# Three plain blocks at the start of the up projection with its differences on VectorE, six banks in the down projection, and output gates later in the chunk steps

## The reference

```python
m = W_out [ retention group | HGRN2 group | sliding-window attention group ](x @ w_in)
x = layernorm(ALPHA * x + m)
h = relu(x @ w_up)                              # w_up is 1024 x 4096
x = layernorm(ALPHA * x + (h * h) @ w_down)     # w_down is 4096 x 1024
```

## Time and profile before

| | |
|---|---|
| median of three executions | 2855.7 us (2853.38 to 2856.41) |
| the profiled execution | 2851.14 us |
| its span | 2849.0 us |
| PE / PEld busy | 2586.0 us (91%) / 2396.6 us (84%) |
| DVE / POOL / ACT busy | 1709.1 us (60%) / 1075.5 us (38%) / 834.9 us (29%) |
| mean granted clock of PE | 0.954 of full |

### The profile page before, as it was taken

The page is one execution under the profiler, slowest core; times in us unless marked ns, Lnnn a source line. Parts: engine busy times, 40 slices in busy tenths (PEclk is TensorE's granted clock), DMA queues, the critical chain, the costliest instruction groups (busy, mean ns, idle before and its releaser), DMA issues. The chain is left out here.

```text
span 2849.0 us, 45428 instructions
## 1 busy us (share of the span) xinstructions
PE 2586.0 (91%) x18174; PEld 2396.6 (84%) x18174; DVE 1709.1 (60%) x3360; ACT 834.9 (29%) x1668; POOL 1075.5 (38%) x1090
## 2 busy tenths in 40 slices
PE   6998888787899999999899988887978999999996
PEld 6997776586899999999899877666868999999986
DVE  2136668557756566666751366785586555666668
ACT  2235456321222221111122445562322222211110
POOL 0027456635455532222000456664535555222220
PEclk9999999888999999999999999997989999999998
DMA  4442222152133352322343422321512333532223
GB/s 156 144 153 82 84 75 76 40 174 78 61 109 103 104 183 91 94 91 91 102 142 127 160 81 68 103 65 30 178 67 88 102 110 99 180 97 91 91 76 108
DMA packets 225889, 295.84 MB, mean 104 GB/s; under 512 B 28816, under 2 KB 177616, under 8 KB 225648
## 3 DMA queue, kind: packets, MB, share of 16 engines
q1 hardware_dynamic: 225680, 292.94, 32.1%
HBM read 217.27 MB, written 77.66 MB: 104 GB/s over the span
## 5 line engine op out<-in xcount | busy, mean ns | idle before, releaser
L1081 PE MATMUL ps<-hid_hi,wd_hi 128*128 128x256 f32 (+2 forms) x800 | 259.3, 324 | 19.9 <-DVE acc_a L2733 13.1
L1081 PE MATMUL ps<-hid_hi,wdl_hi 128*128 128x256 f32 (+2 forms) x800 | 257.8, 322 | 0.0
L1082 PE MATMUL ps<-hid_lo,wdl_hi 128*128 128x256 f32 (+2 forms) x800 | 256.3, 320 | 0.0
L1083 PE MATMUL ps<-hid_hi,wdl_lo 128*128 128x256 f32 (+2 forms) x800 | 256.2, 320 | 0.0
L1082 PE MATMUL ps<-hid_lo,wd_hi 128*128 128x256 f32 (+2 forms) x800 | 255.6, 320 | 0.0
L1083 PE MATMUL ps<-hid_hi,wd_lo 128*128 128x256 f32 (+2 forms) x800 | 255.6, 320 | 0.0
L3038 POOL TENSOR_TENSOR wq_lo_S<-ws,wq_hi_S 128x512 fp32r<-128x512 f32 x112 | 209.2, 1877 | 107.4 <-ACT wq_hi_S L2059 107.4
L2717 DVE TENSOR_TENSOR acc_a<-ps,acc_a 128x512 f32<-128x512 f32 x208 | 143.8, 692 | 152.3 <-PE ps L1083 152.3
L2987 POOL TENSOR_TENSOR wl_lo<-wl_raw,wl_hi 128x2048 fp32r<-128x2048 f32 x14 | 63.8, 4554 | 449.2 <-ACT wl_hi L1772 449.1
L2717 DVE TENSOR_TENSOR acc_b<-ps,acc_b 128x256 f32<-128x256 f32 (+1 forms) x416 | 178.2, 439 | 77.4 <-PE ps L1083 72.1
L1081 PE MATMUL ps<-t_hi_T,wq_hi_S 128*128 128x256 f32 (+1 forms) x672 | 193.2, 288 | 20.0 <-issue 20.0
(11 more groups left out here) (329 smaller groups left out, 7991.9 us busy)
## 6 DMA issues: line engine op xcount, KB each, us to landing
wd_raw<-in_w_down SPq DMA_DIRECT2D x32, 1024.0 KB, 4.9
wq_raw<-in_w_up SPq DMA_DIRECT2D x28, 1024.0 KB, 6.3
wl_raw<-in_w_in SPq DMA_DIRECT2D x20, 1024.0 KB, 5.2
wi_raw<-in_w_in SPq DMA_DIRECT2D x15, 1280.0 KB, 6.4
hidscr<-h SPq DMA_DIRECT2D x32, 544.0 KB, 8.0
out_y<-xn SPq DMA_DIRECT2D x32, 512.0 KB, 4.2
hidscr<-h SPq DMA_DIRECT2D x32, 512.0 KB, 7.2
hid_raw<-hidscr SPq DMA_DIRECT2D x32, 512.0 KB, 3.5
```

The lines of the kernel that those rows point to most:

```text
L1081: nc.tensor.matmul(out, a_hi, b_hi, start=start, stop=False)
L1082: nc.tensor.matmul(out, a_hi, b_lo, start=False, stop=False)
L1083: return nc.tensor.matmul(out, a_lo, b_hi, start=False, stop=stop)
```

## The change: what it does

**Up.** Block 2 becomes a third plain block: `PLAIN = 3`, six more units, 13 blocks of seven products instead of 14. POOL's `side` is gone; DVE makes all four differences and lows of both sides, in an order written anew among the squares. `split_wu(2)` puts the third block's high part on ACT and low part on POOL, each in two halves, into the buffers of block 0. SP loads it ahead of the first quarters. `rectify` of block 2 writes over block 0's h, and waits until that is saved. **Down.** Six banks instead of three; the lows of block 15 are spread over parts 0 and 1. **Chunk steps.** `gates_clip(f)` stands behind `heads_keys` of the chunk's own step, the ACT chain of three (`gates_out`) behind that step's `front_copies`, `front_silu` behind `heads_weights`, and POOL's product with the norm's weights behind `levels`. In step 4 POOL runs `rotate(g)` behind `levels`.

```diff
-         (1, 0, 2), (1, 1, 2), (0, 0, 2), (0, 1, 2)]
+         (0, 0, 2), (0, 1, 2), (1, 0, 2), (1, 1, 2)]
+PLAIN = 3
+UNITS += [(2, f, c) for f in range(2) for c in range(TCH)]
-SEVENS = FBLOCKS - 2
+SEVENS = FBLOCKS - PLAIN
...
# SP
-                load_quarters(l, 2)
+                load_wu(l, 2)                    # waits for wu_hi_done and wu_lo_done of block 0
+                load_quarters(l, PLAIN)
...
+                save_h(l, 0, 1)
                 save_h(l, 1, 1)
-                save_h(l, 0, 1)
...
# PE, up_unit: lows of tokens awaited at the first unit of each token range
+                if b == 0 and f == 0:
                     pe.wait_ge(sd.sem, sd.at("lo", split_no(l, 0, (3, 5, 8)[c])))
# PE, feed
+                for unit in UNITS[8:]:
+                    up_unit(l, *unit)
+                for b in range(PLAIN, FBLOCKS):
                     up(l, b)
# PE, down
-                        if i >= 3:
-                            pe.wait_ge(down_free, n - 2)
+                        if i >= 6:
+                            pe.wait_ge(down_free, n - 5)
...
-                            last = three(ps[:, i % 3, 0:CW[c]], ...
+                            last = three(ps[:, i % 6, 0:CW[c]], ...
# PE, down_last: the first three units
-                        pe.wait_ge(xd.sem, xd.at("h1", seven_no(l, FBLOCKS - 1)))
+                        pe.wait_ge(down_free, DOWN * l + 334 + i)
# ACT, gates
                     nc.scalar.activation(g_r[:], g_r[:], ACT.Ln).then_inc(gh.step("f"), 1)
+
+                def gates_out(c):
                     act.wait_ge(gc.sem, gc.at("c1", c.n))
                     nc.scalar.activation(gate[c.p][:], gate[c.p][:], ACT.Exp, scale=-1.0).then_inc(gh.step("eg"), 1)
...
                         front_copies(f)
+                        gates_out(f)
                     dense(step, "a1")
# ACT, rectify
+                if b == 2:
+                    act.wait_ge(h_saved[0][c > 0], saved(l, 0))
# ACT, weight_high
+                if b == PLAIN:
+                    act.wait_ge(wu_lo_done, 4 * (l + 1))
# ACT, feed, after high(l, 0, 7)
                 rectify(l, 0, 1, 1)
+                high(l, 0, 8)
+                rectify(6); rectify(7); rectify(8); side_high(0, "T2"); rectify(9); split_wu(2)
+                rectify(10); side_high(1, "T2"); rectify(11); side_high(0, "T1"); side_high(1, "T1")
+                rectify(12); weight_high(3, 0..2); rectify(13); weight_high(3, 3); side_high(0, "T3")
+                rectify(14); side_high(1, "T3"); rectify(15); side_high(0, "T4"); rectify(16)
+                side_high(1, "T4"); rectify(17); weight_high(3, 4..5)
# DVE, chunk step
                     if h:
                         heads_keys(h)
                     if f:
-                        front_silu(f)
+                        gates_clip(f, chunk_at(l, step - 2))
...
                         heads_weights(h)
                     if f:
+                        front_silu(f)
                         front_levels(f)
...
                         window_low(f)
-                        if g:
-                            gates_clip(g, h)
# DVE, feed, after low(l, 0, 8)
+                side_t1(0); side_t2(0); square(6); square(7); side_t4(0); side_t1(1); square(8)
+                side_t2(1); side_low(0, "T2"); square(9); side_t4(1); side_low(1, "T2")
+                square(10); square(11); weight_sums(3); side_t3(0); square(12); side_t3(1)
+                side_low(0, "T3"); side_low(0, "T1"); square(13); side_low(1, "T3"); side_low(1, "T1")
+                square(14); square(15); side_low(0, "T4"); square(16); side_low(1, "T4"); square(17)
...
                 collect_last(l, 0, 0, 4)
-                for c in range(TCH):
-                    hid_low(l, FBLOCKS - 1, c)
+                hid_low(l, FBLOCKS - 1, 0)
                 collect_last(l, 0, 4, 8)
-                collect_last(l, 1, 0, 8)
+                collect_last(l, 1, 0, 3)
+                hid_low(l, FBLOCKS - 1, 1)
+                collect_last(l, 1, 3, 6)
+                hid_low(l, FBLOCKS - 1, 2)
+                collect_last(l, 1, 6, 8)
# POOL, chunk step
-                    if g:
+                    if g and step != 4:
                         rotate(g)
...
                         levels(f, h)
+
+                        if step == 4:
+                            rotate(g)
+                        gate_weights(f)
# POOL, feed
-                side(l)
-                for b in range(2, FBLOCKS):
+                split_wu(l, 2)
+                for b in range(PLAIN, FBLOCKS):
```

More of the change, by code:

```diff
@@ L1017, in feed @@
                         load_wd(l, 0)
-                    if b > 2:
-                        for s in range(2):
-                            save_h(l, b - 1, s)
+                    for s in range(2):
+                        save_h(l, b - 1, s)
                 for c in range(TCH):
@@ L2003, in split_wu @@
             def split_wu(l, b):
+                if b == 2:
+                    act.wait_ge(wu_in[0], 16 * (2 * l + 2))
+                    act.wait_ge(up_ready, up_no(l, 0, 1, 2) + 1)
+                    for f in range(2):
+                        cols = slice(f * P, f * P + P)
+                        copy(wu_hi[:, :, cols], wu_raw[:, :, cols]).then_inc(wu_hi_done, 1)
+                    return
                 hi, raw = ((wu_hi, wu_raw), (wu1_hi, wu1_raw))[b]
-                act.wait_ge(wu_in[b], 16 * (l + 1))
+                act.wait_ge(wu_in[b], 16 * ((2 - b) * l + 1))
                 copy(hi[:], raw[:]).then_inc(wu_hi_done, 1)
@@ L2611, in u_part @@
                 return part[:, 4 * int(q[0]) - 4:4 * int(q[0]), at:at + w]
[L2613 to L2616, removed]
-                v.tensor_tensor(tmp[:], u_part(u_lo, "12", 1), u_part(u_lo, "11", 1), ALU.subtract).then_inc(tv.step("t1b"), 1)
-                dve.wait_ge(tv.sem, tv.at("t1b", l))
-                v.tensor_tensor(raw[:], raw[:], tmp[:], ALU.add).then_inc(tv.step("t1"), 1)
@@ new lines, in side_t2, with side_t3 @@
+            def side_t2(l, s):
+                S, raw = tv[s], t_raw[s]["T2"]
+                dve.wait_ge(S.sem, S.at("t1", l))
+                v.tensor_tensor(raw[:], u_part(u_hi, "22", s), t_raw[s]["T1"][:], ALU.subtract).then_inc(S.step("t2a"), 1)
+                dve.wait_ge(S.sem, S.at("t2a", l))
+                v.tensor_tensor(raw[:], raw[:], u_part(u_lo, "22", s), ALU.add).then_inc(S.step("t2"), 1)
+            def side_t3(l, s):
+                if s:
+                    dve.wait_ge(y_out[0], y_stores(l, 0, 8))
+                S, raw, tmp = tv[s], t_raw[s]["T3"], t_tmp[s]["T3"]
+                v.tensor_tensor(raw[:], u_part(u_hi, "22", s), u_part(u_hi, "12", s), ALU.subtract).then_inc(S.step("t3a"), 1)
+                v.tensor_tensor(tmp[:], u_part(u_lo, "22", s), u_part(u_lo, "12", s), ALU.subtract).then_inc(S.step("t3b"), 1)
+                dve.wait_ge(S.sem, S.at("t3b", l))
+                v.tensor_tensor(raw[:], raw[:], tmp[:], ALU.add).then_inc(S.step("t3"), 1)
@@ new lines, in side_t4, with side_low @@
+            def side_t4(l, s):
+                if s:
+                    dve.wait_ge(y_out[1], y_stores(l, 0, 7))
+                S, raw = tv[s], t_raw[s]["T4"]
+                dve.wait_ge(S.sem, S.at("t2", l))
+                v.tensor_tensor(raw[:], u_part(u_hi, "21", s), t_raw[s]["T2"][:], ALU.subtract).then_inc(S.step("t4a"), 1)
+                dve.wait_ge(S.sem, S.at("t4a", l))
+                v.tensor_tensor(raw[:], raw[:], u_part(u_lo, "21", s), ALU.add).then_inc(S.step("t4"), 1)
+            def side_low(l, s, m):
+                dve.wait_ge(ta[s].sem, ta[s].at(m, l))
+                v.tensor_tensor(t_lo[s][m][:], t_raw[s][m][:], t_hi[s][m][:], ALU.subtract).then_inc(tv[s].step(f"l{m}"), 1)
@@ L2823, in _ @@
             g_ = nc.gpsimd
-            for S in (rp, rv, gp, zp, dp, tp):
+            for S in (rp, rv, gp, zp, dp):
                 pool.sem_inc(S.sem, 1)
@@ L2994, in split_wu @@
             def split_wu(l, b):
-                pool.wait_ge(wu_hi_done, 2 * l + b + 1)
+                if b == 2:
+                    for f in range(2):
+                        cols = slice(f * P, f * P + P)
+                        pool.wait_ge(wu_hi_done, 4 * l + 3 + f)
+                        g_.tensor_tensor(wu_lo[:, :, cols], wu_raw[:, :, cols], wu_hi[:, :, cols], ALU.subtract)\
+                            .then_inc(wu_lo_done, 1)
+                    return
+                pool.wait_ge(wu_hi_done, 4 * l + b + 1)
```

217 lines of the change are left out of this document (94 added, 123 removed).

## The result

The changed kernel takes 2752.2 us (median of four, 2746.3 to 2757.1) against 2855.5 of the kernel before: ratio 0.964, interval 0.962 to 0.966, **103 us less**. The forecast was 2763, 93 less, with a range of 2742 to 2816. Its profiled execution took 2746.3 us with a span of 2744.5; that of the kernel before took 2851.1 with a span of 2849.0.

The account below looks back on a forecast made before the run. PE, 91% busy, was taken as the bound, with DVE setting the pace in the start of feed. Up 54, end of down 10 and chunk steps 29 make 93 off 2851.1: 2758, as a median 2763, range 2742 to 2816.

Parts of the forecast that it names:

- up, both layers: First up unit to block 3: most PE idle and some slow clock go, less a third block's cost; 54 us.
- end of down: Last block's lows spread out: PE's wait shrinks and the slow clock behind it goes, 10 us for both layers.
- chunk steps: Chunk steps of mix: PE's waits for g_kt and u_lo shrink through the new orders, 29 us for both layers.
- six banks: Down projection: PE is already full with three banks, so six give 0, bounds 0 and 1 us per layer.
- My sign: End of down: less than 1.5 us of PE wait there would show the forecast right.
- Without it g_kt is earlier by just this: Chunk steps, layer 0: without the clip ahead on DVE, g_kt waits shrink by its delay, 2.1 + 8.4 + 0.4 us.
- The rotation: Step 4: POOL's rotate behind the levels shortens the longest u_lo wait, 4.5 us, bounds 0 and 6.3.
- Rival 1: Chunk steps: the moved clip delays the heads' level work and all 29 us are lost, 2792 or 2806; chance 0.18.
- Rival 2: Up is bound by DVE or a save: 12 us per layer instead of 26.9, 2793; chance 0.18.
- Rival 3: Start of feed and end of down: all idle and slow clock go, 2750; chance 0.07.
- Rival 5: Up's idle only moves to block 3's first products and later waits, within 0.2% of 2856; chance 0.04.
- Rival 4: Up: DVE and POOL's turns follow the moved differences, 2885 if all 28 a layer are slowed; chance 0.05.

Follow-up runs that it names:

- e1: The kernel before with the whole up part alone (third plain block, differences on DVE), mix and down as before: 2804.4 us against 2856.5.
- e3: The kernel before with only block 15's three lows spread over parts 0 and 1 at the end of down: 2845.7 us, ratio 0.996.
- e2: The kernel before with the chunk-step part alone (clip, exponentials, silu and step 4's rotation moved): 2818.0 us, ratio 0.986.
- e4: The kernel before with six banks instead of three in the down projection, nothing else: 2852.2 us, ratio 0.9986.
- e7: The changed kernel with side 0's four differences and lows made by POOL again, three plain blocks kept: 2782.1 us.
- e10: The changed kernel with twelve extra DVE copies of g_kt before PE's awaited one, in steps 2 and 3 of each layer: 2786.0 us.
- e9: The changed kernel run again, unchanged, as a measure for other runs: 2751.9 us, ratio 0.964.

## Why the prediction was right, by its own steps

| term | forecast | measured |
|---|---|---|
| up, both layers | 54 | 52 (e1) |
| end of down | 10 | 10.7 (e3) |
| chunk steps | 29 | 38.5 (e2) |
| six banks | 0 | 4.3 (e4) |
| sum | 93 | 105.5, together 103.3 |

The parts add up within their intervals, so no gain was handed from one to another that these runs could tell. The total came within 11 us of the forecast because three of the four terms are right or small; the one that is not, the chunk steps, makes up most of the difference.

*Up.* The view that DVE paces the start of feed, slowed by POOL's turns, held: e7 shows it by putting the turns back. The third block as the time that the T parts need held too: `issue` is 0.9 instead of 10.0. Of 28.0 idle I left 3.3; 5.5 stayed after, mostly as waits for u_lo, which I had not listed. The busy time, 79.2 and 77.5, was forecast as 77.0 + 2. DVE is busy 76.9 of 84.7 us after, less than PE's 79.2, so it no longer sets the pace of the whole stretch; only the rest of PE's idle time still ends on it. In the 93 us over which I had drawn DVE's schedule (633.21 to 726.20) it is busy 85.2, where I had 88. Blocks 3 to 15 cost 1.1 more per layer; 0.9 of it is the wait at block 3's second product, which I had counted at nothing.

*The end of down.* Right in the sum, and in its two terms (e3). The first wait went whole, and the next ones grew by 1.3. My sign, less than 1.5 us of wait there, holds for the first wait alone, for 5.3 remain behind the residuals.

*The chunk steps* are the mis-sized term. "Without it g_kt is earlier by just this" held: in layer 0 the wait fell by 12.1, where I had 10.9 less 1.0. The rotation is worth less than I said: 5.6 us less wait for u_lo but 2.8 new for rot_k, where I had 4.5. In all, idle time fell by 24.6, forecast 29. What was missing is the clock. I had counted the slow clock behind the gaps in up and at the end of down, and not here, where the granted clock was 0.92 and 0.93 in steps 1 to 4. It gave 13.7 in the profiles, and e10 shows that gaps of this kind cause it.

*The banks* are the step that failed outright, though small: 0 with a bound of 1 per layer; it was 2.2. I had taken "busy" in the window as proof that PE waits for nothing.

*The rivals.* Rival 1 (chunk steps give it back) is out by e2: g_kt's 12 us per layer didn't come back elsewhere; new are only about 3 for the rotation and, in layer 0 of after, 2.6 in the waits for `m` of the window attention (4.0 instead of 1.4), and at times 2.7 for s_prob. Rival 2 (up bound by DVE, half the gain) is out by e1. Rival 3 named 2750, nearer to the measured 2752 than my 2763, but by luck: it wanted all idle time of the start and of down's end gone, and 5.5 and 5.3 us stayed in layer 0. What was gained beyond my forecast came from the chunk steps' clock and the banks. Rival 5 is out, for the products of blocks 3 to 15 grew by 1.1 us only. Rival 4, the slower side, is out: of the moved differences the three beside POOL's lows do take 2.2 to 2.3, and two others 3.4 and 3.5, but the 20 difference instructions of layer 0 after take 32.5 us, 1.6 each, below the 2 that I had named, for POOL is busy only 13.9 of 84.7 us. e7 prices what turns at the wrong place cost, 15 us per layer. So the moment of the turns matters, and not that there are some. The rule of the Trainium skill that I set beside it (*GPSIMD Engine Reference*, section 8, Key points) is that POOL contends with VectorE's instructions that have two SBUF inputs or are in a 2-port mode. The rows of e7 agree for the first kind: `xn`, with two inputs in SBUF, takes 3.44 us beside POOL's differences and 1.28 without. I had named that kind alone, but the clip has one such input and was slowed too, 4.35 us for two instead of 0.48.

What stays open: the rotation's share within 7 to 17 us, and how much beside its own length a gap in the chunk steps costs, which is 1.1 to 3 us by e10's three readings.

## What to carry to other kernels

When an engine's instruction takes 2.7 times its usual length, look which other engine works beside it before counting its work; here moving fourteen instructions a layer onto the busier engine won 26 us, because it ended the turns where PE waited. Where the granted clock of a stretch is below 1, count a gap of PE there at more than its idle time; in the chunk steps of this kernel it was a fifth to a half more. And a stage whose operands come late can be served by putting plain work ahead of it, even if that work is 3 us longer: here it won another 26.

## What the runs showed of the hardware

- Idle gaps of PE of 6 us in a stretch of short matmuls lower the mean granted clock of that stretch: with four gaps of 6.07 us, two a layer, it was 0.93 and 0.92, and without them 0.98 and 0.99 (after) or 0.98 and 0.96 (e9). The same matmuls were busy 11.6 us longer than in after and 7.5 longer than in e9, so 2 to 3 us a gap.
- A PE that the profile shows as busy all the time can hide a short pause, for the records of matmuls overlap. Down's blocks take 23.37 us with three banks and 23.25 with six, both shown as busy; the pause of 0.11 us is seen in the starts of the matmuls. Compare the lengths of equal blocks.
- DVE instructions take longer beside POOL's: `xn` 3.45 us instead of 1.28, and in the same norm one on 128x1 elements (`newt`) 2.35 instead of 0.15. The residual sum, with an input in PSUM, stayed at 1.22.
- The same steps of an unchanged kernel, in five profiles, took 630.3 to 635.6 us in layer 0 and 602.2 to 608.2 in layer 1. The busy time differed by 6.0 and 7.9, for the same matmuls, and the idle time by 1.8 and 4.5. So neither can be compared from one profile where a few us matter.
